# Conv groups moved four half-chunks later, twelve taps for GpSimd, and the solver's data in ten transfers

## The reference

```python
h = rmsnorm(x, g_pre[i])
proj = h @ w_in[i]
qkv, z_a, b_raw, a_raw, glu_in, z_b, gate_logits = jnp.split(proj, _split_points(), axis=-1)
...
o_a = gated_delta_chunked(q, k, v, g, beta)      # 16 heads of 128, chunks of 64
o_a = rmsnorm(o_a, g_dn_out[i]).reshape(B, S, DN_WIDTH).astype(x.dtype) * jax.nn.silu(z_a)
y_a = o_a @ w_br_a[i]

u = jax.nn.glu(glu_in, axis=-1)
u = causal_depthwise_conv(u, w_dw[i]) + b_dw[i]  # 31 taps per channel
u = jax.nn.silu(layernorm(u, ln_g[i], ln_b[i])) * jax.nn.silu(z_b)
y_b = u @ w_br_b[i]
```

```python
A = jnp.einsum('bhnid,bhnjd->bhnij', kb, k) * decay * strict
T = lax.linalg.triangular_solve(eye + A, jnp.broadcast_to(eye, A.shape),
                                left_side=True, lower=True, unit_diagonal=True)
```

## Time and profile before

| | |
|---|---|
| median of 3 runs | 2235.69 us (2234.68 to 2239.55) |
| the profiled execution, its span | 2236.06 us, 2234.2 us |
| busy TensorE, VectorE, ACT, GpSimd | 2151.8, 1494.3, 1224.1, 262.7 us |
| a high piece, a low piece (mean) | 626, 696 ns |
| a tap on VectorE, a product on ACT, an add on GpSimd (mean) | 479, 499, 1018 ns |
| moved by DMA | 431.30 MB, mean 193 GB/s |

### The profile page before, as it was taken

One profiled execution on the slowest core, in us unless ns is written; L12 is line 12 of the kernel. 1 busy time (PEld: TensorE's weight loads), 2 busy tenths in 40 slices (PEclk: granted clock), 3 DMA queues, 4 the chain that ended last, 5 costly groups with the idle time before them and its releaser, 6 DMA issues.

```text
span 2234.2 us, 29331 instructions
## 1 busy us (share of the span) xinstructions
PE 2151.8 (96%) x10062; PEld 1775.3 (79%) x10062; DVE 1494.3 (67%) x2779; ACT 1224.1 (55%) x2356; POOL 262.7 (12%) x385
## 2 busy tenths in 40 slices
PE   7999999999999999999999999999999899999996
PEld 5788888887777778888788887788788688888885
DVE  4778778788999876655765565653466654456665
ACT  4666666676666754445555555544354355555542
POOL 0111111144433431010000000000000000000000
PEclk9999999999999999999999999999999999999998
DMA  5866766778767686665656555565555455654452
GB/s 183 243 196 197 206 195 195 206 195 234 213 185 196 171 253 202 203 214 201 217 197 246 205 206 176 189 209 171 188 185 170 141 190 185 199 161 146 153 206 94
DMA packets 440112, 431.30 MB, mean 193 GB/s; under 512 B 37888, under 2 KB 313488, under 8 KB 438464
## 3 DMA queue, kind: packets, MB, share of 16 engines
q1 hardware_dynamic: 424208, 381.69, 54.9%
q0 software_dynamic: 5920, 26.68, 3.5%
q10 hardware_dynamic: 9872, 21.50, 2.5%
HBM read 406.72 MB, written 23.09 MB: 192 GB/s over the span
## 4 chain that ended last, share of the span: by engine, by line
PE 77%; DVE 13%; SPq 3%; DMA 3%; issue 2%; ACT 2%; POOL 1%; DVEq 0%; ACTq 0%; POOLq 0%
PE pair L439 22%; PE pair L441 22%; PE pair L440 22%; DVE w_lo L419 4%; DVE QB L1018 3%; DMA conv_and_gate<-ubz 2%; SPq L387 1%; PE QA L1412 1%; PE RA L1428 1%; SPq L693 1%; PE RA L586 1%; SPq L654 1%; PE QB L1497 0%; PE QA L1063 0%; DVE o_t L906 0%
## 5 line engine op out<-in xcount | busy, mean ns | idle before, releaser
L419 DVE TENSOR_TENSOR w_lo<-raw,w_hi 128x512 fp32r<-128x512 f32 x1376 | 932.0, 696 | 434.8 <-ACT w_hi L413 432.8
L413 ACT ACTIVATE w_hi<-raw 128x512 fp32r<-128x512 f32 x1376 | 836.5, 626 | 502.9 <-PE pair L441 479.3
L439 PE MATMUL pair<-w_hi,in_hi 128*128 128x512 f32 x2368 | 953.1, 402 | 8.3 <-DVE in_lo L1082 4.2
L441 PE MATMUL pair<-w_hi,in_lo 128*128 128x512 f32 x2368 | 927.6, 392 | 0.0
L440 PE MATMUL pair<-w_lo,in_hi 128*128 128x512 f32 x2368 | 925.7, 391 | 0.0
L439 PEld LDWEIGHTS pair<-w_hi,in_hi 128*128 128x128 f32 x2368 | 447.4, 189 | 98.2 <-DVE in_lo L1082 5.1
L441 PEld LDWEIGHTS pair<-w_hi,in_lo 128*128 128x128 f32 x2368 | 446.7, 189 | 95.9
L440 PEld LDWEIGHTS pair<-w_lo,in_hi 128*128 128x128 f32 x2368 | 447.7, 189 | 88.9 <-issue 1.0
L987 POOL TENSOR_TENSOR acc_p<-acc_p,tap 128x256 f32<-128x256 f32 x128 | 130.3, 1018 | 51.2 <-ACT tap L971 43.8
L1018 DVE SCALAR_TENSOR_TENSOR QB<-upad,cwl,QB 128x256 f32<-128x256 f32 x304 | 133.6, 479 | 0.0
L971 ACT ACTIVATE tap<-upad,cwl 128x256 f32<-128x256 f32 x160 | 79.9, 499 | 13.5 <-POOL acc_p L987 12.8
(11 more groups left out here) (396 smaller groups left out, 1781.1 us busy)
## 6 DMA issues: line engine op xcount, KB each, us to landing
raw<-in_w_in_dram SPq DMA_DIRECT2D x512, 256.0 KB, 3.7
raw<-in_w_in_dram SPq DMA_DIRECT2D x80, 1024.0 KB, 5.1
raw<-in_w_out_dram SPq DMA_DIRECT2D x48, 1024.0 KB, 5.0
raw<-in_w_kv_shared_dram SPq DMA_DIRECT2D x24, 1024.0 KB, 4.9
raw<-in_w_br_a_dram SPq DMA_DIRECT2D x16, 1024.0 KB, 5.8
raw<-in_w_br_b_dram SPq DMA_DIRECT2D x16, 1024.0 KB, 5.6
raw<-in_w_mem_kv_dram SPq DMA_DIRECT2D x16, 1024.0 KB, 4.9
raw<-in_w_ple_gate_dram SPq DMA_DIRECT2D x16, 1024.0 KB, 5.0
```

The source lines that it names most:

```text
L413: act.activation(w_hi[:, u % 2, q % UK], raw[:, u, q % UK], ACT.Copy).then_inc(hi_ready[u], 1)
L419: dve.tensor_tensor(w_lo[:, u % 2, q % UK], raw[:, u, q % UK], w_hi[:, u % 2, q % UK].bitcast(F32), ALU.subtract)\
L439: pe.matmul(o, xh, wh, start=(q == 0), stop=False)
L441: mm = pe.matmul(o, xl, wh, start=False, stop=(q == KC - 1))
```

## The change

- The conv group's steps move: ACT's tanh from hs 1 to 3, VectorE's `glu2` and `z2b` from 2 to 5, TensorE's transposes from 5 to 9, ACT's copies of them from 5 to 10, VectorE's taps start at 10 and not 6. The two closing sums become `group_last_dve` and stand at hs 2 and 3 of the block after.
- GpSimd's chain gets 12 taps and VectorE 19. ACT's 12 products stand at hs 11, 12, 14, 16, 17, 19, 21, 22, 24, 26, 27 and 29.
- The store of group j's `ubz` is issued in block 18 + j at hs 8.
- The solver's steps stand at hs 0, 1, 4, 6, 7, 8 and 9 of a block, ahead of the taps. ACT turns the inverse at hs 5.
- The heads lie in memory in another order (head h at 4 (h mod 4) + h div 4). One load then takes a 32 x 32 block of all 16 heads: 8 loads. The inverse is stored as it lies in SBUF: 2 stores. The loads of the inverse for the rule are as many as before and read 128-byte pieces. For the new order, ACT's loop over the heads 4 to 15 is written out.
- `o_t` is turned at hs 7 on TensorE and copied at 9 on ACT and VectorE.

```diff
-    SOLVE_AT = (2, 5, 9, 13, 17, 21, 28)
+    SOLVE_AT = (0, 1, 4, 6, 7, 8, 9)
...
     def solve_in_sp(sp):
         all_heads_stored(sp)
-        for g in range(NG):
-            for b in range(P // SUB):
-                for tile in range(TT):
-                    at = SUB * g + 8 * b + GROUP * tile
-                    col = tile * S + SUB * b
-                    sp.dma_start(sv_u[at:at + GROUP], ap_dram[GROUP * g:GROUP * (g + 1), SUB * b:SUB * (b + 1), col:col + SUB])\
-                      .then_inc(s["sv_loaded"], 16)
+        for b in range(P // SUB):
+            for tile in range(TT):
+                at, col = SUB * b + HEADS * tile, tile * S + SUB * b
+                sp.dma_start(sv_u[at:at + HEADS], ap_dram[:, SUB * b:SUB * (b + 1), col:col + SUB]).then_inc(s["sv_loaded"], 16)
...
         for k, sv in enumerate((sv_w, sv_u)):
-            for g in range(NG):
-                for b in range(P // SUB):
-                    at = SUB * g + 8 * b
-                    sp.dma_start(t_dram[b, :, k, g].rearrange("r (q i) -> q r i", q=8), sv[at:at + 8]).then_inc(s["t_stored"], 16)
+            sp.dma_start(t_dram[k], sv[:, :, :].rearrange("p r i -> p (r i)")).then_inc(s["t_stored"], 16)
...
     def oa_pe(pe, g, hs):
-        if hs == 1:
+        if hs == 7:
...
     def oa_act(act, g, hs):
-        if hs == 2:
+        if hs == 9:
...
     def oa_dve(dve, g, hs):
-        if hs == 3:
+        if hs == 9:
...
-    POOL_TAPS = 10
+    POOL_TAPS = 12
...
+    ACT_TAP_AT = tuple(11 + 20 * n // POOL_TAPS for n in range(POOL_TAPS))
+
     def group_pe(pe, j, par, hs):
-        if hs == 5:
+        if hs == 9:
             pe.wait_ge(s["glu_ready"], j + 1)
...
-        if hs == 1:
+        if hs == 3:
             act.wait_ge(s["gate_biased"], j + 1)
...
-        if hs == 5:
+        if hs == 10:
             act.wait_ge(s["b_cols"], j + 1)
...
-        if 8 <= hs < 8 + 2 * POOL_TAPS and hs % 2 == 0:
-            n = (hs - 8) // 2
+        if hs in ACT_TAP_AT:
+            n = ACT_TAP_AT.index(hs)
...
-        if hs == 2:
+        if hs == 5:
             dve.wait_ge(s["b_tanh"], j + 1)
...
-        if 6 <= hs < 6 + DVE_TAPS:
-            k = hs - 6
+        if 10 <= hs < 10 + DVE_TAPS:
+            k = hs - 10
...
-        if hs == 30:
+
+    def group_last_dve(dve, j, par, hs):
+        if hs == 2:
             dve.wait_ge(long_tap[0], (DVE_TAPS + 1) // 2 * (j + 1))
             dve.wait_ge(s["pool_taps"], (POOL_TAPS - 1) * (j + 1))
             dve.tensor_tensor(acc[:, :], taps_sum[:, 0:S], acc_p[:, :], ALU.add).then_inc(s["u_summed"], 1)
-        if hs == 31:
+        if hs == 3:
...
-        with act.Fori(4, HEADS, 2) as h:
+        for h in range(4, HEADS, 2):
...
         def others(blk, _, hs):
-            if hs == 4 and blk >= BLK_B + 3:
-                ubz_out_act(act, blk - BLK_B - 3)
+            if hs == 8:
+                ubz_out_act(act, blk - BLK_B - 2)
```

More of the change, by code:

```diff
@@ L126, in program @@
     ex_dram = nc.dram_tensor("values_of_heads", (HEADS, P, EX_END), F32, kind="Internal").ap()
-    t_dram = nc.dram_tensor("inverse_blocks", (P // SUB, SUB, 2, HEADS // GROUP, TT * GROUP * SUB), F32, kind="Internal").ap()
+    t_dram = nc.dram_tensor("inverse_blocks", (2, P, SUB * SUB), F32, kind="Internal").ap()
     ubz_dram = nc.dram_tensor("conv_and_gate", (KC, P, 2, S), F32, kind="Internal").ap()
@@ L603, in scores_act @@
             reach(act, s["ap_stored"], 32 * h)
-            to = lambda a: a[bass.ds(h, 1)].rearrange("a p n -> p (a n)")
-            act.dma_start(to(ap_dram), ap[:, par].rearrange("p t c n -> p (t c n)")).then_inc(s["ap_stored"], 16)
-            act.dma_start(to(ex_dram), ex[:, par, 0:EX_END]).then_inc(s["ap_stored"], 16)
+            at = GROUP * (h % GROUP) + h // GROUP
+            act.dma_start(ap_dram[at], ap[:, par].rearrange("p t c n -> p (t c n)")).then_inc(s["ap_stored"], 16)
+            act.dma_start(ex_dram[at], ex[:, par, 0:EX_END]).then_inc(s["ap_stored"], 16)
     def scores_dve(dve, h, par, hs):
@@ L701, in t_in_sp @@
             rows = slice(SUB * b, SUB * (b + 1))
-            sp.dma_start(to[rows, :, :, rows].rearrange("r t h i -> r (t h) i"), t_dram[b, :, k, g].rearrange("r (q i) -> r q i", q=8))\
+            sp.dma_start(to[rows, :, :, rows].rearrange("r t h i -> r (t h) i"), t_dram[k, SUB * b + g:SUB * (b + 1):GROUP].rearrange("q (r i) -> r q i", r=SUB))\
               .then_inc(s["t_loaded"], 16)
     def head_rows(a, g, at, end):
-        return a[GROUP * g:GROUP * (g + 1), :, at:end].rearrange("h p n -> p h n")
+        return a[g:HEADS:GROUP, :, at:end].rearrange("h p n -> p h n")
     def ap_in_sp(sp, g):
@@ L1774, in beside_act @@
             group_act(act, KC - 1, 1, hs)
[L1775 to L1778, removed]
+        if blk in (BLK_GB, BLK_GB + 1) and hs == 8:
+            ubz_out_act(act, KC - 2 + blk - BLK_GB)
         if blk < BLK_Y:
@@ L1879, in beside_dve @@
             group_dve(dve, KC - 1, 1, hs)
+        if blk in (BLK_GB, BLK_GB + 1):
+            group_last_dve(dve, KC - 2 + blk - BLK_GB, (blk - BLK_GB) % 2, hs)
         if BLK_GB <= done < BLK_GB + 4 and hs == 0:
@@ L2201, in others @@
         def others(blk, _, hs):
-            if hs == 4 and blk >= BLK_B + 3:
-                ubz_out_act(act, blk - BLK_B - 3)
+            if hs == 8:
+                ubz_out_act(act, blk - BLK_B - 2)
             if hs == 1 and blk == SOLVE_BLK:
                 solve_stage_act(act)
-            if hs == 3 and blk == SOLVE_BLK + 9:
+            if hs == 5 and blk == SOLVE_BLK + 9:
                 solve_turn_act(act)
@@ L2238, in solve @@
                     solve_dve(dve, n)
+        last = lambda j, par, hs: group_last_dve(dve, j, par, hs)
         for j in range(2, KC):
-            dve_block(dve, BLK_B + j, beside([(group, j - 1, 1 - j % 2), (solve, BLK_B + j, 0)]))
+            dve_block(dve, BLK_B + j, beside([(group, j - 1, 1 - j % 2), (last, j - 2, j % 2), (solve, BLK_B + j, 0)]))
         tail_dve(dve)
```

4 lines of the change are left out of this document (2 added, 2 removed).

## The result

The changed kernel takes 2203.55 us (median of 4 runs, 2203.43 to 2205.39), beside 2236.58 for the kernel before on the same chip: ratio 0.9853, 95% interval 0.9841 to 0.9864. That is 33.0 us less; 2206.5 was forecast, and 2196 to 2222 as the range. The span of the profiled execution is 2201.8 us against 2234.2, 32.4 less.

What follows compares the result with a forecast made beforehand. TensorE was taken to set the time, except where late VectorE work holds it up. 30.9 (conv waits) - 4 (GpSimd's chain) + 2.6 (rule blocks) = 29.5 us off 2236.06 gives 2206.5 us; range 2196 to 2222.

Steps and rivals of the forecast that it cites:

- The wait of the transposes goes, and 30.9 us with it: Conv blocks 17 to 31: TensorE no longer waits for VectorE at the transposes of `glu2` and `z2b`; 30.9 us back.
- the 22.3 to 23.2 named as the sign: Sign that the forecast is right: blocks 18 to 31 take 22.3 to 23.2 us each.
- its three worst blocks: Blocks 20, 22 and 31, said to carry 2.4 + 5.1 + 7.7 = 15.2 of the 30.9 us lost.
- Ten transfers: SP's queue: ten solver transfers for 64 let `bg` be issued some 4 us before blocks 20 and 31; 22 earlier too.
- under 6 named as the sign: Sign that the forecast is right: solver loads take under 6 us of SP's queue.
- Twelve taps, 4 us: GpSimd's longer chain delays psum copies to 3.6 us into the next conv block; cost 4 us in all, bounds 0 and 9.
- Low pieces blocked by adds, the slower rival: Conv blocks: GpSimd's adds get in before VectorE's low pieces, 5.8 us a block; +41, time 2277; chance 0.04.
- Block 33, a gain of 0.9: Rule block 33: wait at `o_t` goes, 4.7 us wait moves to the product after `level5`; 5.6 - 4.7 = 0.9 gained.
- Blocks 34 to 36: Rule blocks after 33: 34 and 35 wait 0.5 and give 0.4 each, 36 gives 0.9.

Runs made afterwards that it cites:

- steps_only: Kernel before with only the group's steps moved four half-chunks (taps from 10, both closing sums at 31): 2213.44 us, 0.9892 of the kernel before.
- steps_back: Changed kernel with tanh, gates, transposes and their copies at their old half-chunks, taps still starting at 10: 2207.99 us, 0.9863 of the kernel before.
- dma64: Changed kernel with the solver transfers cut into 32 loads and 32 stores again: 2204.62 us, 0.9847 of the kernel before.
- pool14: Changed kernel with fourteen taps on GpSimd's chain and 17 on VectorE: 2219.48 us, 0.9913 of the kernel before.
- vec_early: Changed kernel with the load of `vec` issued after group 2, last closing sums at half-chunk 6, sums of block results at 4: 2199.03 us, 0.9822 of kernel before.
- dma_only: Kernel before with only the ten solver transfers, the new head order and the unrolled loop: 2228.57 us, 0.9957 of the kernel before.
- sums_back: Changed kernel with the two closing sums back at half-chunks 30 and 31 of the group's own block: 2204.04 us, 0.9848 of the kernel before.

## Why the prediction was right, and where not

**The wait of the transposes goes, and 30.9 us with it: right.** 30.17 + 0.66 = 30.8 came back in blocks 17 to 31, and the blocks 18 to 31 came out at 22.23 to 22.26 us, just under the 22.3 to 23.2 named as the sign. The order of causes was only half seen. The text gave the wait to the move of four half-chunks, with the rest as support. steps_only confirms 24 us for the move, but steps_back shows that the rest, the later taps among it, does nearly the same work without it. Put alone into the kernel before, the transfers give 10 us, the earlier store of `ubz` 12 to 15 and the move of the steps 24 to 26. That is half as much again as there was to lose: they are not terms of a sum, but feed one chain, in which a delay pushes VectorE's taps into the next block and meets the next delay there, as blocks 21 and 22 show. The prediction counted block 22 among those that a late `bg` holds up; VectorE did not wait for `bg` there. And its three worst blocks are not the worst: block 27 (694.90 to 721.18, 26.28 us) lost 4.0, block 20 only 2.4.

**Ten transfers: right for blocks 20 and 31 of the kernel before, worth little in the changed one.** `bg` was issued 3.6 us before block 20 and 4.0 before block 31 (4 forecast). In dma64 only block 20 still pays, 1.5 us, though with quicker stores than the old ones. The text did not ask what the transfers are worth once the other cures are in, and it looked at `bg` alone where ACT waited up to 6.6 us for weights behind the same transfers. The eight loads took 6.0 us of the queue, 5 forecast and under 6 named as the sign.

**Twelve taps, 4 us: mis-sized, it is 0.** The forecast let the first add start 2.7 us later, four half-chunks. It starts 9.96 us into block 18 where it was 8.13, so 1.8 later: ACT's second tap, which it needs, moved from half-chunk 10 to 12 only. The pace of 1.385 us was right (1.36 forecast). The ninth add ends 21.6 us into the block, not 22.9, the copies 2.1 us into the next and not 3.6, and the gates are ready at 6.55, not 7.8. pool14 puts the copies at 4.8 and pays 16.3 us in blocks 18 to 31.

**Low pieces blocked by adds, the slower rival: did not come.** In the stretch of taps of block 25 all of VectorE's low pieces take 0.68 to 0.69 us and the adds up to 1.32. So GpSimd gives way there, as the forecast had argued from block 18. Only pieces at the start of a block, out of step with the taps, are stretched (1.23 once in block 25). The Trainium skill's page "SBUF — State Buffer", section "SBUF: two separate sides", has one engine hold the shared port pair for a whole instruction. The traces agree with that: an add takes 0.74 us alone and 1.22 to 1.32 where a low piece is in progress, and a low piece that meets an add takes 1.23 us and not 0.68.

**Block 33, a gain of 0.9: wrong, a loss of 2.75.** GpSimd and VectorE in that block, which begins at 826.19:

```profile
826.82 0.79 POOL L1989 DMA_DIRECT2D vec<-in_b_gate_dram  x1
...
828.66 1.67 POOL L855 TENSOR_TENSOR orn<-orn,halfpow 128x8 f32<-128x8 f32 x1
```

```profile
830.37 2.19 DVE L900 SCALAR_TENSOR_TENSOR o_t<-o_t,orn,zs 128x128 f32<-128x128 f32 x8 [4.51 <-POOL orn L855]
...
834.92 1.41 DVE L1885 SCALAR_TENSOR_TENSOR gst<-pair,small,vec 128x512 f32<-128x512 f32 x2 [1.16 <-DMA vec<-in_b_gate_dram]
...
837.64 0.68 DVE L862 TENSOR_TENSOR x<-RA,const 128x512 f32<-128x512 f32 x1
```

The place was right (the wait moved to the product that needs `x`), and the power was ready 4.1 us into the block, 3.9 forecast. Two things failed. The load of `vec` stands in GpSimd's queue behind the adds, and VectorE waits 1.16 us for it: a DMA moved with its engine's queue that the walk left out. So `x` ends 12.1 us into the block and not 10.6, and TensorE waits 5.9 us and not 4.7. And the subtraction "5.6 - 4.7" took all of 5.6 as a wait that goes. The wait was 4.0, and it ended with group 15's closing sum and not with `o_t` (TensorE's waits in the kernel before, 823 to 900 us):

```profile
PE QA L813 <- DVE ubz L1027: 4.0, 1, 4.0
```

The other 1.6 was TensorE being busy for 38.15 us in that block at a clock of 0.96. After the longer wait the clock is at 0.92 and the busy time 39.02. So the loss of 2.75 is 1.9 more of waiting and 0.9 more of being busy. vec_early moves that load and the sums out of the way and gets 4.7 us back, 2.2 of them as busy time (39.02 - 36.84).

**Blocks 34 to 36: right in kind, small in size.** 0.76, 0.91, 1.09 against 0.4, 0.4, 0.9.

**The sum.** 30.9 - 4 + 2.6 = 29.5 was forecast; 30.8 - 0 + 0.0 (2.76 in blocks 34 to 36, less 2.75 in 33) = 30.8 is what the edits did in the profile, and block 40's clock adds 1.7. The two errors, 4 us and 2.6 us, stood on opposite sides, so that the total came so near is partly luck. The mechanism that carries it, the wait of the transposes, is the one forecast.

**Open.** Which part of the change makes VectorE ready without the move (two taps fewer, the sums and solver steps placed elsewhere, the store, or the later taps) was not separated; solver steps, sums and taps can each be put back alone at no cost that could be measured. Nor is it known what decides between the two clocks of block 40.

## What to carry to other kernels

Undoing one part of a change shows what that part is worth with the others there, and two cures for one wait hide each other; run one part alone in the old kernel as well before calling it the cause. When work is added to an in-order queue, walk everything behind it, loads included, to who waits for it: here one load behind the added adds had its share in the only block that got clearly slower. And ask for the point at which a chain of two engines stops fitting its block (here between twelve and fourteen taps), since under it the work is free and above it most blocks pay.

## What the runs showed of the hardware

GpSimd's 256-column adds settled into VectorE's rhythm, one per 1.385 us though one alone takes 0.74, while adds of half the columns took 0.56 on the mean and were paced by their input instead. After a wait of 3 to 6 us in front of TensorE the granted clock of the stretch was 0.88 to 0.96 (3.4 us and 0.94 in block 22 of the kernel before, 3.6 and 0.88 in that of dma_only, 4.7 and 0.96 in block 33 of sums_back, 5.9 and 0.92 in block 33 here), so the length of the wait alone does not give it; after two waits of 1.7 us it stayed at 1.00 (vec_early). And block 40, the same instructions in every kernel, was seen at 1.00 and at 0.93, 23.9 and 25.5 us, among kernels that differ only well before it: 1.6 us that no edit explains.
